# A three-layer transformer kernel: the up projections of layer 0 as one stream with the first scores among them, key rotation on GpSimd, squares of x0 to x3 folded to 256 columns

## The chip, the core and the metric

The kernel runs as one launch on one core of one Trainium2 chip. The metric is device time in microseconds, 991.06 us as the median of 3 runs of the kernel before (990.77 to 992.12). All weights are read from device memory once, as float32.

## What is computed

Two blocks are computed one after the other on 256 tokens of 1024 features. The change touches layer 0 of the first block, whose mixer is latent attention, and the norms before the projections of both layers. Cut to that:

```
x0 = x
h = rms_norm(x, g);  a = h @ w_a;  cq, ckv, kr = split(a, [384, 640])
q  = (rms_norm(cq,  g_q ) @ w_uq ).reshape(B, S, 8, 128 + 64)
kv = (rms_norm(ckv, g_kv) @ w_ukv).reshape(B, S, 8, 128 + 128)
q_rope = apply_rope(q[..., 128:]);  k_rope = apply_rope(kr)     # 64 wide, k_rope shared by the heads
s = (q_nope . k_nope + q_rope . k_rope) * 192 ** -0.5
y = softmax(mask(s)) @ v @ w_o
x1 = x + rms_norm(y, g);  z = swiglu(rms_norm(x1) )
x2 = x1 + rms_norm(z, g);  layer 1 likewise gives x3 and x4
```

An rms norm needs the sum of squares over the features, and features lie on partitions, so each such sum is a matmul with a matrix of ones.

## The kernel before

Activations lie transposed, features on the 128 partitions and the 256 tokens along the row. Every weight tile is 128 x 128 (a *unit* here). To keep float32 accuracy, a weight unit is used as a high part and a low part: ScalarE rounds it to `whi` (line 883), VectorE subtracts to give `wlo` (line 1343), and TensorE issues three matmuls of 256 columns for each unit, high x high, high x low and low x high (lines 495, 496, 501; for values with tokens as output rows, lines 550, 551, 556, of 512 columns for four units at once). The activation has the same two parts (`cqh`, `cql`; `oh`, `ol`).

Weights arrive in *pieces* of 16 units, in the order of the table `STREAM`, through four raw buffers and three buffers for the two parts. SyncE issues the load of a piece when VectorE has made the low parts of the piece four before it. ScalarE makes high parts of a piece when TensorE has used up the piece three before it. In layer 0 pieces 4 to 8 are `wuk` (keys, 16 units), `wuq` (queries, 16), `wuv` (values, 16), `wuq` (16), `wuq` (4). Pieces 9 to 12 are `wo0`.

Every engine has its own program, written out in order, with semaphore waits between them. In layer 0 all four engine programs walk one list that `_order0` and `_mixed` make (lines 141 to 195): it runs over the projection units and puts the attention steps of the four head pairs among them where a credit and a distance in units allow it. The steps of a pair are `scores` (line 625), softmax (`biased`, `exps`, `normal`), `turn` (the transposes, line 635), `values` (line 651) and `chunk` (lines 941 and 1425), which gives two units' worth of input for `wo0`. Before that list TensorE does all of `wuk` by itself, and then the list starts with 16 units of `wuq` and 6 of the 8 token blocks of `wuv`, before the first scores.

VectorE evicts a projection from PSUM with the norm's factor (`scaled_out`, lines 1436), two chunks of 256 columns at a time. Rotation of keys and of queries is `rotate`, six VectorE instructions of 256 columns (lines 1446 to 1453). The sum of squares: ScalarE makes the squares of pairs of feature chunks (128 x 512), VectorE adds them up (`square_sum`, line 1373), and TensorE multiplies the 512 columns by ones in two float32 matmuls of 256 columns (line 591). For y and z sums a `fold` (line 1379) first adds the two halves on VectorE, so one matmul does. Where token-wise factors are wanted as well (`columns`, lines 602 to 605), four matmuls of one column follow.

## Time and profile before

The profiled execution took 990.73 us, and its span of instructions 988.6 us, so 2.1 us lie around it. The median of the runs is 0.33 us above the profiled execution.

| stretch (us) | what | TensorE busy | VectorE busy | ScalarE busy | granted clock |
|---|---|---|---|---|---|
| 0 to 988.6 | all | 959.7 (97%) | 721.8 (73%) | 542.7 (55%) | 0.997 |
| 10 to 20 | first projection | 7.55 | 6.49 | 6.99 | 0.84 |
| 33.37 to 51.92 | up projections | 18.25 of 18.55 | 18.34 | 9.62 | 1.00 |
| 51.92 to 76.27 | attention among the rest of them | 20.76 of 24.35 | 16.25 | 10.23 | 1.00 |
| 76.27 to 108.34 | attention among the output projection | 31.57 of 32.07 | 17.00 | 16.64 | 1.00 |

GpSimd is busy for 17.3 us of the whole span. A share of busy time is an average over stages, so the table is to be read by stage. A matmul's record is longer than the distance to the next one, because matmuls are pipelined: in a steady row a record is 0.28 us and the next starts 0.12 us after it.

### The profile page before, as it was taken

To read this page: it belongs to the slowest core of one execution; us is meant where nothing else is said; L and a number is where in the kernel's file an instruction comes from. 1 tells how busy PE (TensorE), PEld (TensorE's weight loads), DVE (VectorE), ACT (ScalarE), POOL (GpSimd) and SP (SyncE) were. 2 spreads that over 40 slices of the span, in tenths; PEclk is the share of its full clock that TensorE was granted. 3 is DMA by queue.
4 is the path that set the end of the run, shared out by engine and by line. 5 is a ranking of instruction groups with operands and counts; after the bars stand their busy time and mean duration, and the time that the engine had idled before them with its cause. 6 is when DMAs were issued, how large, how long until landed. Compare 5 with 4: busy or idle time off the path is not lost.

```text
span 988.6 us, 18855 instructions
## 1 busy us (share of the span) xinstructions
PE 959.7 (97%) x7951; PEld 923.9 (93%) x7951; DVE 721.8 (73%) x1342; ACT 542.7 (55%) x837; POOL 17.3 (2%) x48
## 2 busy tenths in 40 slices
PE   6999999999999999999999999999999999999997
PEld 6978999999998988799999998898999999999996
DVE  5965788887657877699878888646654879888653
ACT  6635565454436556565545444546755567676542
POOL 0000000000000000000000000000130000000000
PEclk9999999999999999999999999999999999999999
DMA  7433467676664742438666883543333545555521
GB/s 288 182 128 128 193 221 280 225 252 259 263 212 154 269 147 109 171 146 323 247 265 256 328 317 122 214 175 125 129 131 130 209 171 186 199 185 199 212 89 43
DMA packets 28452, 194.71 MB, mean 197 GB/s; under 512 B 3280, under 2 KB 3536, under 8 KB 5456
## 3 DMA queue, kind: packets, MB, share of 16 engines
q1 hardware_dynamic: 28368, 193.51, 52.7%
q8 instruction: 63, 1.03, 0.4%
q14 instruction: 21, 0.17, 0.0%
HBM read 192.45 MB, written 1.05 MB: 196 GB/s over the span
## 4 chain that ended last, share of the span: by engine, by line
PE 85%; DVE 7%; ACT 5%; issue 2%; DMA 1%; SPq 1%; POOL 0%; DVEq 0%; ACTq 0%
PE bank L495 24%; PE bank L496 23%; PE bank L501 23%; DVE s_wlo L1343 2%; PE bank L625 2%; PE bank L651 2%; ACT s_whi L883 2%; PE bank L556 2%; PE bank L550 2%; PE bank L551 1%; PE bank L515 1%; PE bank L522 1%; PE bank L516 1%; PE bank L635 1%; DMA s_raw<-in_wa 1%
## 5 line engine op out<-in xcount | busy, mean ns | idle before, releaser
L1343 DVE TENSOR_TENSOR s_wlo<-s_raw,s_whi 128x512 fp32r<-128x512 f32 (+1 forms) x364 | 371.3, 1061 | 141.1 <-ACT s_whi L883 140.7
L883 ACT ACTIVATE s_whi<-s_raw 128x1024 fp32r<-128x1024 f32 (+2 forms) x233 | 305.3, 1336 | 212.2 <-PE bank L501 198.2
L495 PE MATMUL bank<-s_hh,s_whi 128*128 128x256 f32 x1400 | 393.6, 281 | 0.4 <-DVE s_hl L1425 0.2
L496 PE MATMUL bank<-s_hl,s_whi 128*128 128x256 f32 x1400 | 387.6, 277 | 0.0
L501 PE MATMUL bank<-s_hh,s_wlo 128*128 128x256 f32 x1383 | 382.8, 277 | 0.0
L495 PEld LDWEIGHTS bank<-s_hh,s_whi 128*128 128x128 f32 x1400 | 263.3, 188 | 6.2 <-issue 5.1
L496 PEld LDWEIGHTS bank<-s_hl,s_whi 128*128 128x128 f32 x1400 | 263.1, 188 | 0.1
L501 PEld LDWEIGHTS bank<-s_hh,s_wlo 128*128 128x128 f32 x1383 | 259.8, 188 | 0.0
L495 PE MATMUL bank<-s_ph,s_whi 128*128 128x256 f32 x528 | 146.4, 277 | 0.0
L496 PE MATMUL bank<-s_pl,s_whi 128*128 128x256 f32 x528 | 145.8, 276 | 0.0
L501 PE MATMUL bank<-s_ph,s_wlo 128*128 128x256 f32 x516 | 142.5, 276 | 0.0
L496 PEld LDWEIGHTS bank<-s_pl,s_whi 128*128 128x128 f32 x528 | 99.2, 188 | 0.0
L495 PEld LDWEIGHTS bank<-s_ph,s_whi 128*128 128x128 f32 x528 | 99.2, 188 | 0.0
L501 PEld LDWEIGHTS bank<-s_ph,s_wlo 128*128 128x128 f32 x516 | 96.9, 188 | 0.0
L1358 DVE CUSTOM_DVE_ANT_0 s_raw<-s_raw,s_adacc 128x1024 f32<-128x1024 f32 x48 | 56.8, 1221 | 0.0
L515 PE MATMUL bank<-s_hh,s_whi 128*128 128x256 f32 x160 | 41.8, 294 | 11.6 <-DVE s_wlo L1343 7.1
L515 PEld LDWEIGHTS bank<-s_hh,s_whi 128*128 128x128 f32 x160 | 31.7, 198 | 12.8 <-issue 7.7
L516 PE MATMUL bank<-s_hh,s_wlo 128*128 128x256 f32 x160 | 40.8, 288 | 0.0
L495 PE MATMUL bank<-s_oh,s_whi 128*128 128x256 f32 x128 | 36.9, 288 | 2.4 <-DVE s_ol L1425 2.2
L1594 DVE TENSOR_TENSOR s_tmp<-bank,s_R 128x256 f32<-128x256 f32 x44 | 18.6, 422 | 26.2 <-PE bank L501 21.0
L496 PE MATMUL bank<-s_ol,s_whi 128*128 128x256 f32 x128 | 35.8, 280 | 0.0
L501 PE MATMUL bank<-s_oh,s_wlo 128*128 128x256 f32 x128 | 35.8, 280 | 0.0
(237 smaller groups left out, 1278.9 us busy)
## 6 DMA issues: line engine op xcount, KB each, us to landing
s_raw<-in_gu SPq DMA_DIRECT2D x44, 1024.0 KB, 4.9
s_raw<-in_dn SPq DMA_DIRECT2D x33, 1024.0 KB, 4.8
s_raw<-in_wada SPq DMA_DIRECT2D x24, 1024.0 KB, 5.1
s_raw<-in_up SPq DMA_DIRECT2D x22, 1024.0 KB, 4.8
s_raw<-in_wo SPq DMA_DIRECT2D x8, 1024.0 KB, 4.8
...
```

Of the source, the lines that this page charges most:

```text
L495: e.matmul(out, hi, xh[:, k, :], start=first, stop=False, skip_group_check=True)
L496: e.matmul(out, hi, xl[:, k, :], start=False, stop=False, skip_group_check=True)
L501: m = e.matmul(out, lo, xh[:, k, :], start=False, stop=last, skip_group_check=True)
L515: e.matmul(out, hi, xh[:, k, :], start=k == 0 and j % 2 == 0, stop=False, skip_group_check=True)
L516: e.matmul(out, lo, xh[:, k, :], start=False, stop=False, skip_group_check=True)
L550: e.matmul(out, xh[:, k, xk], hi, start=k == 0, stop=False)
L556: m = e.matmul(out, xl[:, k, xk], hi, start=False, stop=k == nk - 1)
L625: m = e.matmul(pair_banks[a][:, cols_], x[:, blk * P:(blk + 1) * P], y[:, 0:rows], start=i == 0 and blk == 0, stop=last, skip_group_check= ...
L651: m = e.matmul(out, v, probs[:, a, keys], start=first, stop=kb == 1, skip_group_check=True)
L883: e.activation(whi[w % SPLIT][:, at], raw[p % RAW][:, at], ACT.Copy).then_inc(S.hi.tick((w, c0)), 1)
L1343: e.tensor_tensor(wlo[s][:, at], raw[p % RAW][:, at], whi[s][:, at].bitcast(F32), ALU.subtract).then_inc(S.lo.tick((i, j), (i, "all")), 1)
L1358: m = e.tensor_tensor_reduce(out=src, in0=src, in1=cact[:, :], scale=1.0, scalar=0.0, op0=ALU.mult, op1=ALU.add, accum_out=modv[:, j:j + 1])
```

## The change

Five things change.

The pieces 4 to 8 now hold one list `MLA` of 68 units in the order in which they are used: 4 `wuk`, 12 `wuq`, 4 `wuk`, 12 `wuq`, 16 `wuv`, 4 `wuk`, 6 `wuq`, 4 `wuk`, 6 `wuq`. Sizes and number of the pieces are as before. Only the first four units of `wuk` stand ahead of the list of steps.

The steps of the pairs are placed by other paces and distances (`PACE0`, `PAIR0`, `AFTER0`). The list was up to the first scores: 16 `wuq`, 6 token blocks of `wuv`; it is: 12 `wuq` (4 to 15 of the stream), 4 `wuk`, 8 `wuq`. The sums for q stand after three units of `wuq`.

The keys' rotation leaves VectorE and is six GpSimd instructions, with one wait between the first four and the last two, and a semaphore of its own.

VectorE makes the low parts of the third piece of the stream ahead of the first eviction of `wuk`.

For x0, x1, x2 and x3 VectorE folds the two halves, and TensorE has one matmul where it had two; for x2 also two matmuls of one column where it had four.

```diff
-STREAM = [("wa", 56), ("wuk", 16), ("wuq", 16), ("wuv", 16), ("wuq", 20), ("wo0", 64), ("gu0", 352), ("dn0", 176),
+MLA = ([("wuk", i) for i in range(4)] + [("wuq", i) for i in range(12)] +
+       [("wuk", i) for i in range(4, 8)] + [("wuq", i) for i in range(12, 24)] + [("wuv", i) for i in range(16)] +
+       [("wuk", i) for i in range(8, 12)] + [("wuq", i) for i in range(24, 30)] +
+       [("wuk", i) for i in range(12, 16)] + [("wuq", i) for i in range(30, 36)])
+STREAM = [("wa", 56), ("mla", 68), ("wo0", 64), ("gu0", 352), ("dn0", 176),
...
+PACE0 = {"wuk": 0.72, "wuq": 0.84, "wuv": 0.2, "wo0": 0.26}
+PAIR0 = (18, 18, 44, 44)
+AFTER0 = {**AFTER, "exp": ("scores", 9), "scale": ("exp", 3), "values": ("turn1", 7), "chunk": ("values", 0)}
...
             tiles("wuk", 0, 2, 2, cqh, cql, "cq", 4, S.dve_out)
             sums("kv", 6, columns=True)
-            tiles("wuk", 2, 2, 2, cqh, cql, "cq", 5, S.dve_out)
-            sums("q", 7)
-            for n in (4, 6):
-                tiles("wuk", n, 2, 2, cqh, cql, "cq", (0, 1)[n // 2 - 2], S.dve_out)
...
+                    if i == 3:
+                        sums("q", 7)
...
-                    q.wait_ge(S.rot, "k")
+                    q.wait_ge(S.rot_k, "k")
...
-                        sums({0: "x1", 1: "x3"}[layer], 0)
+                        sums({0: "x1", 1: "x3"}[layer], 0, acc=1)
...
-            q.wait_ge(S.dve_out, ("cq", 6))
-            rotate(tmp[3][:, :], tmp[4][:, :], A0.K[:, 8, :], A0.K[:, 9, :], "k")
             lo_all(_used_up("wa", 48) + SPLIT)
-            for n in (0, 2, 4, 6):
-                scaled_out("wuk", n, 2, Rs[1], "kv", lambda m: A0.K[:, m, :])
-                if n == 2:
-                    lo_all(_used_up("wa", 56) + SPLIT)
+            lo_all(_used_up("wa", 56) + SPLIT)
+            scaled_out("wuk", 0, 2, Rs[1], "kv", lambda m: A0.K[:, m, :])
...
             for i, b in ((1, 0), (2, 3), (3, 2)):
                 square_sum("x3", i, sqb[b])
+            fold("x3")
             lo_all(_used_up("gu1", 16) + SPLIT)
...
+            q.wait_ge(S.dve_out, ("cq", 6))
+            e.tensor_tensor(tmp[0][:, :], tmp[4][:, :], sinb, ALU.mult)
+            e.tensor_tensor(tmp[1][:, :], tmp[3][:, :], sinb, ALU.mult)
+            e.tensor_tensor(A0.K[:, 8, :], tmp[3][:, :], cosb, ALU.mult)
+            e.tensor_tensor(A0.K[:, 9, :], tmp[4][:, :], cosb, ALU.mult).then_inc(S.rot_k.tick("products"), 1)
+            q.wait_ge(S.rot_k, "products")
+            e.tensor_tensor(A0.K[:, 8, :], A0.K[:, 8, :], tmp[0][:, :], ALU.subtract)
+            e.tensor_tensor(A0.K[:, 9, :], A0.K[:, 9, :], tmp[1][:, :], ALU.add).then_inc(S.rot_k.tick("k"), 1)
```

How instructions stand now. First VectorE between the last part of the first projection (`s_tmp<-bank3`) and the queries' eviction (`s_Q0<-bank2` is the chunks that are rotated; `s_K0` are keys). In the kernel before:

```order
L1520 TENSOR_TENSOR s_tmp<-bank3,s_R0 128x256 x2
L1446 TENSOR_TENSOR s_tmp<-s_tmp,s_adacc 128x256
L1447 TENSOR_TENSOR s_tmp<-s_tmp,s_adacc 128x256
L1449 TENSOR_TENSOR s_K0<-s_tmp,s_adacc 128x256
L1450 TENSOR_TENSOR s_K0<-s_tmp,s_adacc 128x256
L1452 TENSOR_TENSOR s_K0<-s_K0,s_tmp 128x256
L1453 TENSOR_TENSOR s_K0<-s_K0,s_tmp 128x256
L1343 TENSOR_TENSOR s_wlo2<-s_raw1,s_whi2 128x512 x4
L1436 TENSOR_TENSOR s_K0<-bank4,s_R1 128x256 x2
L1436 TENSOR_TENSOR s_K0<-bank5,s_R1 128x256 x2
L1343 TENSOR_TENSOR s_wlo0<-s_raw2,s_whi0 128x512 x4
L1436 TENSOR_TENSOR s_K0<-bank0,s_R1 128x256 x2
```

In the changed kernel at the same place:

```order
L1545 TENSOR_TENSOR s_tmp<-bank3,s_R0 128x256 x2
L1367 TENSOR_TENSOR s_wlo2<-s_raw1,s_whi2 128x512 x4
L1367 TENSOR_TENSOR s_wlo0<-s_raw2,s_whi0 128x512 x4
L1460 TENSOR_TENSOR s_K0<-bank4,s_R1 128x256 x2
L1460 TENSOR_TENSOR s_Q0<-bank2,s_R2 128x256 x2
L1470 TENSOR_TENSOR s_tmp<-s_Q0,s_adacc 128x256
L1471 TENSOR_TENSOR s_tmp<-s_Q0,s_adacc 128x256
L1473 TENSOR_TENSOR s_Q0<-s_Q0,s_adacc 128x256
L1474 TENSOR_TENSOR s_Q0<-s_Q0,s_adacc 128x256
L1476 TENSOR_TENSOR s_Q0<-s_Q0,s_tmp 128x256
L1477 TENSOR_TENSOR s_Q0<-s_Q0,s_tmp 128x256
L1460 TENSOR_TENSOR s_Q0<-bank3,s_R2 128x256 x2
```

The six rotation rows of the keys are gone, eight weight parts stand in one row, and of the four evictions of keys ahead of the queries' first one is left; the other three stand further down.

TensorE around the first scores (`s_K,s_Q`), of before, with a token block of `wuv` (lines 550 to 556) ahead of them and another behind:

```order
L550 MATMUL bank<-s_whi,s_cqh 128x512 [waits dve_evicted]
L551 MATMUL bank<-s_wlo,s_cqh 128x512
L556 MATMUL bank<-s_whi,s_cql 128x512
L625 MATMUL bank<-s_K,s_Q 128x128 [waits rope_made,dve_evicted]
L625 MATMUL bank<-s_K,s_Q 128x128
L625 MATMUL bank<-s_K,s_Q 128x256 x2
L625 MATMUL bank<-s_K,s_Q 128x128 x2
L625 MATMUL bank<-s_K,s_Q 128x256 x2
L625 MATMUL bank<-s_K,s_Q 128x128 x2
L625 MATMUL bank<-s_K,s_Q 128x256 x2
L550 MATMUL bank<-s_whi,s_cqh 128x512 [waits weight_low_made]
```

and of the changed kernel, where a unit of `wuq` stands ahead of them and four more units and then all of `wuv` behind (what was line 625 is 642 now):

```order
L511 MATMUL bank<-s_cqh,s_whi 128x256
L512 MATMUL bank<-s_cql,s_whi 128x256
L517 MATMUL bank<-s_cqh,s_wlo 128x256
L642 MATMUL bank<-s_K,s_Q 128x128 [waits rope_made,key_rope_made,dve_evicted]
L642 MATMUL bank<-s_K,s_Q 128x128
L642 MATMUL bank<-s_K,s_Q 128x256 x2
L642 MATMUL bank<-s_K,s_Q 128x128 x2
L642 MATMUL bank<-s_K,s_Q 128x256 x2
L642 MATMUL bank<-s_K,s_Q 128x128 x2
L642 MATMUL bank<-s_K,s_Q 128x256 x2
L511 MATMUL bank<-s_cqh,s_whi 128x256 [waits weight_low_made]
```

The first scores moved ahead of the token blocks, and wait for one more semaphore, that of the rotated keys.

VectorE at the squares of x3, of before and of the changed kernel (`s_wlo2<-s_raw0` is the fourth piece of the first matrix of the feed-forward part, `s_tmp<-bank5` its first output):

```order
L1358 ISA s_raw3,s_modv<-s_raw3,s_adacc 128x1024
L1358 ISA s_modv 128x1
L1373 TENSOR_TENSOR s_sqacc0<-s_sqacc0,s_yb 128x512 x3
L1343 TENSOR_TENSOR s_wlo2<-s_raw0,s_whi2 128x2048
L1594 TENSOR_TENSOR s_tmp<-bank5,s_R2 128x256
```

```order
L1382 ISA s_raw3,s_modv<-s_raw3,s_adacc 128x1024
L1382 ISA s_modv 128x1
L1397 TENSOR_TENSOR s_sqacc0<-s_sqacc0,s_yb 128x512 x3
L1403 TENSOR_TENSOR s_sqacc0<-s_sqacc0 128x256
L1367 TENSOR_TENSOR s_wlo2<-s_raw0,s_whi2 128x2048
L1622 TENSOR_TENSOR s_tmp<-bank5,s_R2 128x256
```

A fold stands between the square sums and the weight piece.

## Rows read from the trace of the kernel before

**Rows 1.** Who TensorE waited for, whole span: total us, times, longest.

```profile
PE bank L495 <- DVE s_ol L1425: 2.2, 2, 1.8
...
PE bank L625 <- DVE s_Q L1436: 2.1, 3, 1.3
```

**Rows 2.** TensorE in time order: start, us, line, [idle before it].

```profile
16.90 0.55 PE L515 MATMUL bank<-s_hh,s_whi 128*128 128x256 f32 x1 [2.29 <-ACT s_hh L1000]
...
33.37 0.28 PE L495 MATMUL bank<-s_cqh,s_whi 128*128 128x256 f32 x1
...
34.79 1.03 PE L591 MATMUL bank<-s_sqacc,s_ones 128*128 128x256 f32 x4
...
47.31 0.40 PE L550 MATMUL bank<-s_whi,s_cqh 128*128 128x512 f32 x1
...
51.92 3.09 PE L625 MATMUL bank<-s_K,s_Q 128*128 128x128 f32 x24 [0.31 <-DVE s_Q L1436]
...
76.27 0.38 PE L495 MATMUL bank<-s_oh,s_whi 128*128 128x256 f32 x1 [1.79 <-DVE s_ol L1425]
```

**Rows 3.** VectorE in time order, from the first squares to the first scores.

```profile
23.72 3.70 DVE L1343 TENSOR_TENSOR s_wlo<-s_raw,s_whi 128x512 fp32r<-128x512 f32 x6
...
35.14 0.75 DVE L1520 TENSOR_TENSOR s_tmp<-bank,s_R 128x256 f32<-128x256 f32 x2
...
38.19 2.49 DVE L1343 TENSOR_TENSOR s_wlo<-s_raw,s_whi 128x512 fp32r<-128x512 f32 x4
...
40.60 1.41 DVE L1436 TENSOR_TENSOR s_K<-bank,s_R 128x256 f32<-128x256 f32 x4
...
47.47 0.75 DVE L1436 TENSOR_TENSOR s_Q<-bank,s_R 128x256 f32<-128x256 f32 x2
...
50.52 0.68 DVE L1343 TENSOR_TENSOR s_wlo<-s_raw,s_whi 128x512 fp32r<-128x512 f32 x1
```

**Rows 4.** ScalarE: the high parts of the piece that is used third.

```profile
37.47 1.99 ACT L883 ACTIVATE s_whi<-s_raw 128x1024 fp32r<-128x1024 f32 x2
```

**Rows 5.** GpSimd in time order: instructions that read SBUF.

```profile
403.15 1.95 POOL L1927 TENSOR_SCALAR_AFFINE_SELECT s_bias<-s_bias 128x2048 f32<-128x2048 f32 x1 [294.51 <-DMA s_bias<-in_relm]
...
706.44 0.59 POOL L1931 TENSOR_SCALAR_AFFINE_SELECT s_S<-s_S 128x128 f32<-128x128 f32 x1 [3.94 <-ACT s_S L1235]
...
709.04 0.29 POOL L1933 TENSOR_SCALAR_AFFINE_SELECT s_PT<-s_PT 128x128 f32<-128x128 f32 x1
```

**Rows 6.** VectorE beside and away from GpSimd's selects.

```profile
700.60 1.02 DVE L1798 TENSOR_TENSOR s_PT<-s_S,s_PT 128x384 f32<-128x384 f32 x2
...
706.19 1.38 DVE L1343 TENSOR_TENSOR s_wlo<-s_raw,s_whi 128x512 fp32r<-128x512 f32 x2
...
707.49 1.20 DVE L1798 TENSOR_TENSOR s_PT<-s_S,s_PT 128x384 f32<-128x384 f32 x2
...
714.16 1.30 DVE L1343 TENSOR_TENSOR s_wlo<-s_raw,s_whi 128x512 fp32r<-128x512 f32 x2
```

**Rows 7.** TensorE: sums of x2 and x3, and the matmul behind each.

```profile
315.86 1.02 PE L591 MATMUL bank<-s_sqacc,s_ones 128*128 128x256 f32 x4
...
317.54 0.48 PE L550 MATMUL bank<-s_whi,s_hh 128*128 128x512 f32 x1
...
435.52 1.03 PE L591 MATMUL bank<-s_sqacc,s_ones 128*128 128x256 f32 x4
...
436.69 0.36 PE L495 MATMUL bank<-s_hh,s_whi 128*128 128x256 f32 x1
```

**Rows 8.** VectorE: a fold, and what follows the square sums of x1 to x3.

```profile
109.40 0.42 DVE L1379 TENSOR_TENSOR s_sqacc<-s_sqacc 128x256 f32<-128x256 f32 x1
...
132.55 0.42 DVE L1594 TENSOR_TENSOR s_tmp<-bank,s_R 128x256 f32<-128x256 f32 x1 [3.72 <-issue]
...
320.92 2.50 DVE L1343 TENSOR_TENSOR s_wlo<-s_raw,s_whi 128x512 fp32r<-128x512 f32 x4 [3.15 <-ACT s_whi L883]
...
434.25 2.29 DVE L1343 TENSOR_TENSOR s_wlo<-s_raw,s_whi 128x2048 fp32r<-128x2048 f32 x1
```

More of the change, by code:

```diff
@@ L138, in _stick_steps, with _mixed @@
             yield "keep", p
-def _mixed(units, steps, paces, pair_at, chunk_name, per=1):
+def _mixed(units, steps, paces, pair_at, chunk_name, per=1, after=AFTER):
     steps, ahead, at, made, credit = iter(steps), [], {}, set(), 0.0
@@ L159, in ready @@
         else:
-            need, tiles = (AFTER[name][0], i), AFTER[name][1]
+            need, tiles = (after[name][0], i), after[name][1]
         return need in at and n >= at[need] + tiles
@@ L192, in _order0 @@
 def _order0():
-    units = _units("wuq")[:16] + [("wuv", g) for g in range(8)] + _units("wuq")[16:] + _units("wo0")
-    return _mixed(units, _soft_steps(range(4)), {"wuq": 0.3, "wuv": 0.6, "wo0": 0.3},
-                  lambda p: ("wuq", (17, 29, 35)[p - 1]) if p else ("wuv", 0), "wo0", 2)
+    units = [(name, i // 2 if name == "wuv" else i) for name, i in MLA[4:] if name != "wuv" or i % 2 == 0] + _units("wo0")
+    return _mixed(units, _soft_steps(range(4)), PACE0, lambda p: units[PAIR0[p]], "wo0", 2, AFTER0)
 def _order1():
@@ L573, in tokens @@
                     if k == 2 and norm is not None:
-                        sums(norm, 4, columns=True)
+                        sums(norm, 4, acc=1, columns=True)
             def sums(s, b, late=(), acc=2, columns=False):
@@ L602, in sums @@
                     for b in range(2):
-                        e.matmul(out[:, T + b:T + b + 1], sq[:, b * P:(b + 1) * P], ones[:, 0:1], start=True, stop=False)
-                        m = e.matmul(out[:, T + b:T + b + 1], sq[:, T + b * P:T + (b + 1) * P], ones[:, 0:1],
-                                     start=False, stop=True)
+                        for half in range(acc):
+                            at = half * T + b * P
+                            m = e.matmul(out[:, T + b:T + b + 1], sq[:, at:at + P], ones[:, 0:1], start=half == 0,
+                                         stop=half == acc - 1)
                 m.then_inc(S.sums.tick(s), 1)
@@ L684, in tensor_program @@
             for step, i in _order0():
-                if step == "wuq":
+                if step == "wuk":
+                    n, k = i // 2, i % 2
+                    if n % 2 == 0 and k == 0:
+                        bank_of["wuk", n] = (4, 0, 1, 3)[n // 2]
+                        take(bank_of["wuk", n], S.dve_out, ("wuk", n))
+                    q.wait_ge(S.xlo, ("cq", k))
+                    product("wuk", i, banks[bank_of["wuk", n - n % 2]][:, (n % 2) * T:(n % 2 + 1) * T], cqh, cql, k,
+                            k == 0, k == 1, ("wuk", n - 1) if n % 2 == 1 and k == 1 else None)
+                elif step == "wuq":
                     n, k = i // 3, i % 3
+                    if i == 3:
+                        sums("q", 7)
                     if n % 2 == 0 and k == 0:
-                        bank_of["wuq", n] = (2, 3, 0, 1, 2, 3)[n // 2]
+                        bank_of["wuq", n] = (2, 3, 1, 2, 0, 2)[n // 2]
                         take(bank_of["wuq", n], S.dve_out, ("wuq", n))
@@ L1510, in vector_program @@
                 square_sum("x0", i, sqv[i])
+            fold("x0")
             lo_all(_used_up("wa", 16) + SPLIT)
```

53 lines of the change are left out of this document (36 added, 17 removed).

## The prediction

> **What bounds the kernel now.** I read the table of stretches first, then the waits, then the time order of each engine. TensorE is busy for 97% of the span, so time can only come from three places: matmuls that go, waits of TensorE that go, and clock. The waits in the stage that the change rewrites are few: TensorE waits three times for evicted queries (2.1 us in all, the longest 1.3) and twice for the low part of the attention output (2.2 in all, the longest 1.8) [rows 1]. A unit costs 0.353 us: four stand between 33.37 and 34.79 (1.42 us), so 0.118 for each matmul, while a record is 0.28 long [rows 2]. A gap that is printed as idle is thus about 0.16 us longer in truth, and the five waits cost 4.3 + 5 x 0.16 = 5.1 us. This is all that a better order of the stage can give, since its matmuls stay the same.
>
> Who makes TensorE late? Up to 51.92 VectorE has no pause, and the scores wait for it [rows 2, 3]: it does the keys' rotation, the evictions and all low parts ahead of the queries that the first scores need. Behind 51.92 the queries' evictions stand behind softmax work. The longest wait, 1.79 at 76.27, is another thing: ScalarE copies twice and VectorE subtracts, with no work for TensorE beside it.
>
> **The stage, step by step.** Both kernels are alike up to the sums for kv. Up to 47.31 TensorE had 28 units and the sums for q behind them; ahead of the first scores it now has 24 units and the same sums. So it comes to the scores at 47.31 - 4 x 0.353 = 45.9 [rows 2]. What stands ready then?
>
> VectorE: its last eviction of the first projection begins at 35.14 and takes two steps of 0.34 us. The fold of x0 ahead of it costs 0.42 (at 109.40 [rows 8]), so it is free at 36.2. Then eight low parts of 0.60 each (a row of four is 2.49 long, of which 0.09 is the tail of the last, at 38.19 [rows 3]) to 41.0; ScalarE has the last high parts at 37.47 + 1.99 = 39.5, ahead of the seventh part, no wait [rows 4]. Keys out, two steps of 0.34 (four take 1.41 less the tail [rows 3]): 41.7. Queries out and rotated: 50.52 - 47.47 = 3.05, so 44.75 [rows 3]. The next queries out, 0.75: 45.5, and with the semaphore 45.6. That is 0.3 us ahead of TensorE. In the kernel before the same eviction came 0.31 + 0.16 us late although TensorE came 5.5 us later: four evictions, the rotation and weight parts went first.
>
> GpSimd: it starts at 36.2 and must be done by 45.9, so it has 9.7 us for six instructions. The trace has none of their kind. The nearest rows are selects with one input: 128 columns in 0.29 us, 2048 columns in 1.95, so 0.86 ns for each column and 0.18 fixed [rows 5]. Two inputs of 256 columns are between 0.40 (one pass) and 0.62 (two passes); the longest row, 1.95, is the upper end. Beside VectorE instructions with two SBUF inputs a select took 0.59 in place of 0.29 [rows 5, 6], so 0.3 more for each. I take 0.62 + 0.3, and 5.5 us for six, done near 41.8. The keys are not late.
>
> What does VectorE pay? In the same rows 6 its instructions beside four selects took 1.38 against 1.30 and 1.20 against 1.02: 0.26 us for four selects, 0.065 each. A select reads 128 columns once; a product reads 256 twice, four times as much. I take 0.26 each, 1.6 us for six; the low end is 6 x 0.065 = 0.4, the high end that VectorE stands still for all of each, 6 x 0.62 = 3.7. All six fall beside the eight low parts, which have both inputs in SBUF. With 1.6 the scores wait 1.6 - 0.3 = 1.3 us (0.1 to 3.4).
>
> The Trainium skill (SBUF — State Buffer, "Who interferes with whom") says that a VectorE instruction with two SBUF inputs contends with a GpSimd instruction that reads SBUF, and that the winner holds the shared pair for its whole instruction. By that rule the price is the high end. The rows agree that both engines get slower, 0.29 to 0.59 and 1.02 to 1.20, but not that VectorE loses all of it. The same skill (GPSIMD Engine Reference, 3.1) gives 4497 ns for a sum of 2048 columns; scaled to 256 that would be an estimate of 0.56 us, no run here shows it.
>
> Further on, with durations of rows and the new order. The turn of pair 0 comes 1.4 us behind the second scores and needs VectorE's reads of their banks, 768 columns, at 0.34 us for 256 some 1.0 us, more with four instructions, and semaphores: 0.2 late. The third scores come when the eviction of their queries ends: 0.1. The first unit of the output projection needs the chunk of pair 0. Before, TensorE stood 1.79 + 0.16 us there with nothing beside it [rows 2]; now four units, 1.4 us, stand beside the same chain, so 0.5 is left. The fourth turn needs its bank freed behind seven weight parts: 0.1. In sum 0.9 (0.3 to 1.6).
>
> Stage: -5.1 + 1.3 + 0.9 = -2.9 us. SyncE's loads have the same sizes and wait for the same distances, and the low parts that release them come earlier, so I put nothing there. Key rotation on TensorE's side costs nothing but the wait above.
>
> **The folds.** Two float32 matmuls of 256 columns take 1.03 us less the tail of 0.16, 0.87, so one is 0.43 [rows 7]. Behind the sums of x2 the next matmul starts at 317.54, 1.68 after the first: 0.81 for four matmuls of one column, and two of them go, 0.4. The fold costs VectorE 0.42.
> x0: the six low parts at 23.72 follow the squares [rows 3], and the first of them is needed right behind the sums. It comes 0.42 later, so what TensorE saves it waits away: 0 (-0.4 to +0.2).
> x1: VectorE has 3.72 us of idle time behind it, up to 132.55 [rows 8]: -0.43.
> x2: 3.15 us of idle time, up to 320.92 [rows 8]: -0.43 - 0.4 = -0.83.
> x3: here the cover is gone already. The sums start at 435.52 and the next unit should follow at 436.39, but it starts at 436.69 [rows 7], just behind the weight piece that VectorE begins at 434.25 and ends at 434.25 + 2.29 = 436.54 [rows 8]. The fold moves that piece 0.42 later. TensorE saves 0.43 and then waits 0.3 + 0.43 + 0.42: the unit comes 0.4 later than before. +0.4, low end -0.43 if that unit doesn't wait for the piece.
> In sum -0.9.
>
> **Sum.** 990.73 - 2.9 - 0.9 = 986.9 us for an execution like the profiled one (its span 988.6 and 2.1 around it), and 0.3 more for the median: 987.2 us.
>
> **Rivals.**
> A. GpSimd and VectorE shut each other out for whole instructions. For it: the select's 0.59. Against it: VectorE's 0.26 us for four. VectorE is late by 3.7 and the scores by 3.4; if the clock falls as it did at 16.90, where after 2.29 us without work a matmul took 0.55 us in place of 0.28, the level of 1.2 GHz [rows 2], up to 1.6 us more is lost in the next 3.3 us. Sum -5.1 + 3.4 + 0.9 - 0.9 = -1.7: 989.4, with the clock 991.
> B. The softmax chain becomes the bound. ScalarE now makes eight high parts' worth of weights (four instructions of 1.0 us) ahead of the third pair's exponentials, and a turn, a bank or a chunk comes later than I placed it. For it: the slacks that I found there are 0 to 0.3 us. Against it: the long chains have units beside them. At 1.5 us: 988.7.
> C. The slower side: the rotated keys come late. The place is the first scores, the price is 1 us for each us past 45.9, and nothing else of the stage is ready to be done in the meantime, since the matmuls stand in order. At 1.95 us for each, the longest GpSimd row, and 0.3 to 0.6 lost to VectorE, six take 15 us and end at 51.3: 5.4 late, with the clock 7. Then -5.1 + 7 + 0.9 - 0.9 = +1.9: 993.2. It decides from 2.2 us for one instruction on. Against it: two inputs of 256 columns are 512 columns, a quarter of that row.
> D. All goes better: 0.4 us of contention, x0 gives 0.4, the small waits 0.3. -5.1 + 0.1 + 0.3 - 1.3 = -6.0: 985.1.
>
> **How the numbers follow.** The forecast 0.52 (986 to 988.5), A 0.18, B 0.12, C 0.06, D 0.12. The range from 985.0 to 991.0 leaves out C, half of the clock's case of A, and a little beyond D: some 0.13. This kernel's measurement tells a change of about 2 us, 0.2%, from none. Faster than 989.1: the forecast, D, B mostly, and a third of A, 0.75. Within: the rest of A and B, and a part of C, 0.20. Slower: 0.05.
>
> **What the changed profile would show.** Right: the first scores near 46 to 47.5 with VectorE's query eviction as their releaser; low parts in rows longer than 0.62 while GpSimd works between 36 and 42; the last unit of the output projection 2.9 us ahead of before; the matmul behind the sums of x3 waiting about 1.1 us, those of x1 and x2 not. Wrong: scores released by GpSimd; a wait in the chunk of pair 0 as long as before; TensorE at 1.2 GHz near 50 us; or the matmul behind the sums of x3 close behind them.

## The result and the profile after

The changed kernel takes 986.57 us in the median of 7 runs (985.39 to 989.32), the kernel before 990.77 (989.57 to 992.12) beside it. The ratio is 0.9964, with a 95% interval of 0.995 to 0.9977. In a second comparison, with 11 runs of the change, it is 0.9966 (0.9954 to 0.9978). Forecast were 987.2 us and "faster". One run of all, of the kernel with the keys' rotation on VectorE (1389.34 us at a granted clock of 0.65), was in a slow state and is left out. The profiled execution took 986.47 us (forecast 986.9), its span is 983.3 us.

The line numbers have moved. In the kernel after, L511, L512 and L517 are the matmuls of a unit (L495, L496 and L501 before), L607 and L621 the sums of squares, L642 the scores, L1367 the low parts, L1460 the evictions of keys and queries.

Who TensorE waited for from 10 to 110 us, in the kernel after (us in total, times, longest), against [rows 1]:

```profile
PE bank L607 <- DVE s_sqacc L1403: 1.8, 1, 1.8
PE bank L642 <- DVE s_Q L1460: 1.4, 1, 1.4
...
PE bank L511 <- DVE s_ol L1449: 0.4, 1, 0.4
```

Three waits for queries have become one, two waits for the low part of the attention output one, and there is a new one at the sums of x0. In time order TensorE shows (start, us, line, idle before it), against [rows 2]:

```profile
23.69 0.67 PE L607 MATMUL bank<-s_sqacc,s_ones 128*128 128x256 f32 x2 [1.82 <-DVE s_sqacc L1403]
24.20 0.38 PE L511 MATMUL bank<-s_hh,s_whi 128*128 128x256 f32 x1
...
35.46 1.03 PE L607 MATMUL bank<-s_sqacc,s_ones 128*128 128x256 f32 x4
...
47.80 1.36 PE L642 MATMUL bank<-s_K,s_Q 128*128 128x128 f32 x7 [1.35 <-DVE s_Q L1460]
...
73.91 0.38 PE L511 MATMUL bank<-s_oh,s_whi 128*128 128x256 f32 x1 [0.42 <-DVE s_ol L1449]
...
105.83 1.13 PE L612 MATMUL bank<-s_yb,s_ones 128*128 128x256 f32 x4 [0.69 <-ACT s_yb L927]
```

From the sums for kv (35.46) to the first sums for y0 (105.83) the stage takes 70.37 us. Before it took 74.52 (34.79 to 109.31). That is 4.15 of the 5.3 us by which the span is shorter; the folds at x1 and x2 give 1.4 (behind the sums of x1 0.43, behind those of x2 1.00); at the start 0.7 us went the other way, since the sums for kv come 11.77 us behind those of x0 and came 10.77 behind them before, with those of x0 0.3 earlier. The last 0.4 lies behind the sums of z1. The profiled times are only 4.3 us apart, since 3.2 us lie around the span in place of 2.1. There the granted clock was at its lower level, 1.2 GHz, at another place: before right behind the wait at 16.90 [rows 2], after in the stretch from 25 us on. The table of stretches of the kernel after (us, then busy time and instructions of PE, PEld, DVE, ACT and POOL, then the granted clock, DMA share, GB/s):

```profile
25.00:29.00 4.00, 4.00 (x24) 4.00 (x23) 3.70 (x9) 2.15 (x6) 0.00 (x0) 0.58 0.51 143
...
35.46:47.80 12.34, 10.99 (x90) 10.59 (x89) 11.04 (x22) 5.59 (x8) 8.13 (x6) 1.00 0.53 190
```

VectorE up to the first scores, in the kernel after, against [rows 3] (`s_wlo` are low parts, `s_K` and `s_Q` evictions of keys and queries):

```profile
35.53 2.48 DVE L1367 TENSOR_TENSOR s_wlo<-s_raw,s_whi 128x512 fp32r<-128x512 f32 x4
39.22 4.15 DVE L1367 TENSOR_TENSOR s_wlo<-s_raw,s_whi 128x512 fp32r<-128x512 f32 x4 [1.20 <-ACT s_whi L906]
43.29 0.74 DVE L1460 TENSOR_TENSOR s_K<-bank,s_R 128x256 f32<-128x256 f32 x2
...
47.00 0.75 DVE L1460 TENSOR_TENSOR s_Q<-bank,s_R 128x256 f32<-128x256 f32 x2
```

And GpSimd, which rotates the keys beside it:

```profile
35.77 2.85 POOL L1956 TENSOR_TENSOR s_tmp<-s_tmp,s_adacc 128x256 f32<-128x256 f32 x1 [33.23 <-DVE s_tmp L1545]
38.58 0.73 POOL L1957 TENSOR_TENSOR s_tmp<-s_tmp,s_adacc 128x256 f32<-128x256 f32 x1
39.27 1.25 POOL L1958 TENSOR_TENSOR s_K<-s_tmp,s_adacc 128x256 f32<-128x256 f32 x1
40.48 1.19 POOL L1959 TENSOR_TENSOR s_K<-s_tmp,s_adacc 128x256 f32<-128x256 f32 x1
41.74 1.07 POOL L1961 TENSOR_TENSOR s_K<-s_K,s_tmp 128x256 f32<-128x256 f32 x1
42.78 1.20 POOL L1962 TENSOR_TENSOR s_K<-s_K,s_tmp 128x256 f32<-128x256 f32 x1
```

Four low parts took 2.48 us while one GpSimd instruction lasted 2.85, then four took 4.15 while GpSimd needed 1.07 to 1.25 for each. The one instruction in which VectorE stood idle took 0.73. That is the puzzle for the experiments. The second row comes 1.20 us late because of ScalarE, whose high parts of this piece stand behind a function that waits for TensorE's sums for kv (L621):

```profile
37.31 0.48 ACT L934 ACTIVATE s_L<-bank,s_epsc 128x258 f32<-128x258 f32 x1 [2.07 <-PE bank L621]
...
38.15 1.99 ACT L906 ACTIVATE s_whi<-s_raw 128x1024 fp32r<-128x1024 f32 x2
```

The sums of x2 and x3 in the kernel after, against [rows 7]:

```profile
311.80 0.59 PE L607 MATMUL bank<-s_sqacc,s_ones 128*128 128x256 f32 x2
312.23 0.50 PE L621 MATMUL bank<-s_ones,s_sqacc 128*128 128x1 f32 x4
312.59 0.47 PE L566 MATMUL bank<-s_whi,s_hh 128*128 128x512 f32 x1
...
430.67 0.59 PE L607 MATMUL bank<-s_sqacc,s_ones 128*128 128x256 f32 x2
432.09 0.36 PE L511 MATMUL bank<-s_hh,s_whi 128*128 128x256 f32 x1 [0.83 <-DVE s_wlo L1367]
```

From the sums of x2 to the next matmul it is 0.79 us (1.68 before). From those of x3 it is 1.42 (1.17 before).

### The profile page after: what moved, and what is told of

It reads as the page before. It is cut to its first block, busy times and chain, and to the rows that moved or that the text cites. A ratio compares the mean times of both kernels' runs of the same rounds, so it can differ in the third digit from the quotient of the medians.

```text
span 983.3 us, 18834 instructions
## 1 busy us (share of the span) xinstructions
PE 954.9 (97%) x7939; PEld 920.2 (94%) x7939; DVE 722.6 (73%) x1340; ACT 542.3 (55%) x837; POOL 25.4 (3%) x54
## 4 chain that ended last, share of the span: by engine, by line
PE 88%; ACT 4%; DVE 4%; issue 1%; DMA 1%; SPq 1%; POOL 0%; DVEq 0%; ACTq 0%
PE bank L511 25%; PE bank L512 24%; PE bank L517 23%; PE bank L642 2%; PE bank L668 2%; PE bank L572 2%; PE bank L566 2%; ACT s_whi L906 2%; PE bank L567 2%; DVE s_wlo L1367 1%; PE bank L531 1%; PE bank L538 1%; PE bank L532 1%; PE bank L652 1%; DMA s_raw<-in_wa 1%
## 5 line engine op out<-in xcount | busy, mean ns | idle before, releaser
L1367 DVE TENSOR_TENSOR s_wlo<-s_raw,s_whi 128x512 fp32r<-128x512 f32 (+1 forms) x364 | 372.7, 1065 | 141.6 <-ACT s_whi L906 141.4
L511 PE MATMUL bank<-s_hh,s_whi 128*128 128x256 f32 x1400 | 394.1, 282 | 1.2 <-DVE s_wlo L1367 0.8
L512 PE MATMUL bank<-s_hl,s_whi 128*128 128x256 f32 x1400 | 388.1, 277 | 0.0
L517 PE MATMUL bank<-s_hh,s_wlo 128*128 128x256 f32 x1383 | 383.4, 277 | 0.0
L511 PEld LDWEIGHTS bank<-s_hh,s_whi 128*128 128x128 f32 x1400 | 263.9, 189 | 7.5 <-issue 6.2
L512 PEld LDWEIGHTS bank<-s_hl,s_whi 128*128 128x128 f32 x1400 | 264.0, 189 | 0.1
L517 PEld LDWEIGHTS bank<-s_hh,s_wlo 128*128 128x128 f32 x1383 | 260.5, 188 | 0.0
L511 PE MATMUL bank<-s_ph,s_whi 128*128 128x256 f32 x528 | 146.4, 277 | 0.0
L512 PE MATMUL bank<-s_pl,s_whi 128*128 128x256 f32 x528 | 145.8, 276 | 0.0
L517 PE MATMUL bank<-s_ph,s_wlo 128*128 128x256 f32 x516 | 142.5, 276 | 0.0
L512 PEld LDWEIGHTS bank<-s_pl,s_whi 128*128 128x128 f32 x528 | 99.2, 188 | 0.0
L511 PEld LDWEIGHTS bank<-s_ph,s_whi 128*128 128x128 f32 x528 | 99.2, 188 | 0.0
L517 PEld LDWEIGHTS bank<-s_ph,s_wlo 128*128 128x128 f32 x516 | 96.9, 188 | 0.0
L531 PE MATMUL bank<-s_hh,s_whi 128*128 128x256 f32 x160 | 40.4, 288 | 10.9 <-DVE s_wlo L1367 7.5
L511 PE MATMUL bank<-s_oh,s_whi 128*128 128x256 f32 x128 | 36.8, 287 | 0.6 <-DVE s_ol L1449 0.4
L512 PE MATMUL bank<-s_ol,s_whi 128*128 128x256 f32 x128 | 35.7, 279 | 0.0
L517 PE MATMUL bank<-s_oh,s_wlo 128*128 128x256 f32 x128 | 35.7, 279 | 0.0
```

What stands on the lines that cost most here:

```text
L511: e.matmul(out, hi, xh[:, k, :], start=first, stop=False, skip_group_check=True)
L512: e.matmul(out, hi, xl[:, k, :], start=False, stop=False, skip_group_check=True)
L517: m = e.matmul(out, lo, xh[:, k, :], start=False, stop=last, skip_group_check=True)
L531: e.matmul(out, hi, xh[:, k, :], start=k == 0 and j % 2 == 0, stop=False, skip_group_check=True)
L1367: e.tensor_tensor(wlo[s][:, at], raw[p % RAW][:, at], whi[s][:, at].bitcast(F32), ALU.subtract).then_inc(S.lo.tick((i, j), (i, "all")), 1)
```

## The experiments

All are edits of the changed kernel. Single times scatter by one or two us, more than most of the effects, so the main measure is a length in the trace of one profiled execution of each kernel: the stage from the sums for kv to those for y0, and the wait ahead of the first scores in it.

| kernel | median us (runs) | ratio to before (95% interval) | stage us | wait at first scores, printed |
|---|---|---|---|---|
| before | 990.77 (7) | 1 | 74.52 | 0.31 |
| changed | 986.57 (7) | 0.9964 (0.9950 to 0.9977) | 70.37 | 1.35 |
| changed, again | 987.60 (11) | 0.9966 (0.9954 to 0.9978) | 74.11 | 1.85 |
| keys' rotation on VectorE | 988.93 (10, ratio from 9) | 0.9980 (0.9970 to 0.9991) | 71.37 | 2.08 |
| no rotation of keys | 985.00 (4) | 0.9939 (0.9924 to 0.9953) | 68.97 | none |
| early GpSimd product | 985.86 (6) | 0.9954 (0.9939 to 0.9969) | 70.99 | 1.82 |
| later parts | 984.30 (4) | 0.9934 (0.9919 to 0.9949) | 69.04 | none |
| later parts, rotation on VectorE | 984.32 (5) | 0.9937 (0.9925 to 0.9949) | 69.05 | none |
| no folds | 986.40 (8) | 0.9966 (0.9954 to 0.9978) | 70.69 | 1.55 |
| no fold x0, x3 | 985.63 (12) | 0.9957 (0.9945 to 0.9969) | 75.86 | 1.90 |
| later parts, no fold x0, x3 | 983.29 (5) | 0.9926 (0.9914 to 0.9938) | 69.08 | none |
| later parts, no fold x0 | 983.88 (5) | 0.9928 (0.9915 to 0.9941) | 69.00 | none |
| later parts, no folds | 985.30 (5) | 0.9938 (0.9924 to 0.9952) | 69.03 | none |

The stages of 74.11 and 75.86 hold a stretch at 1.2 GHz, of which more below. Without a wait at the scores the stage is 68.97 to 69.08 us in all six kernels; what it is longer in the other kernels with the new order, but for these two, is their wait, within 0.3 us.

**Keys' rotation back on VectorE.**

```diff
+            q.wait_ge(S.dve_out, ("cq", 6))
+            rotate(tmp[3][:, :], tmp[4][:, :], A0.K[:, 8, :], A0.K[:, 9, :], "k")
             lo_all(_used_up("wa", 48) + SPLIT)
...
-            e.tensor_tensor(A0.K[:, 9, :], A0.K[:, 9, :], tmp[1][:, :], ALU.add).then_inc(S.rot_k.tick("k"), 1)
```

> The keys' rotation goes back to VectorE, right behind the last eviction of the first projection; all else is as in the changed kernel. Theory S (the two engines share, and each gets slower): VectorE gains 1.66 us, since its second row of four low parts takes 2.49 again in place of 4.15, and the 1.20 us that it stood idle ahead of that row take up half of the 2.3 us of the rotation. Then evictions, rotation of the queries and the first scores come 0.5 us earlier than in the changed kernel: scores at 47.3, a printed wait of 0.8 us in place of 1.35. The time is that of the changed kernel or 0.5 us less (986.0 to 986.6). Rival R (the move to GpSimd took 2.3 us off VectorE, as it was meant to): the scores come 1 to 2.3 us later, wait 2.3 to 3.6, time 987.5 to 989.

VectorE in this kernel:

```profile
35.22 0.75 DVE L1545 TENSOR_TENSOR s_tmp<-bank,s_R 128x256 f32<-128x256 f32 x2
...
38.27 4.89 DVE L1367 TENSOR_TENSOR s_wlo<-s_raw,s_whi 128x512 fp32r<-128x512 f32 x8
...
46.80 0.74 DVE L1460 TENSOR_TENSOR s_Q<-bank,s_R 128x256 f32<-128x256 f32 x2
```

From the end of the first projection's evictions to the second eviction of queries VectorE needed 10.9 us (35.89 to 46.80), against 11.47 in the changed kernel (35.53 to 47.00), of which 1.20 are the idle time. But the two profiles differ in their start. Here the sums for kv came at 34.40, 10.4 us behind those of x0, and not 11.8, so the scores waited longer, 2.08. The fair partner is the changed kernel run again (further down), which has its sums at the same place and no idle time: there VectorE needed 10.55 us (36.01 to 46.56) and the scores waited 1.85. Of the 2.4 us that the rotation takes on VectorE, 2.0 come back, because the rotation of the queries no longer meets GpSimd. So beside a like execution the move to GpSimd is worth 0.2 to 0.4 us. Theory S's gain could only come in an execution with the idle time; that was not profiled with this kernel. The wait is above S's 0.8 and below rival R's 2.3 to 3.6. The median, 988.93, is at the upper end of R's 987.5 to 989; nine runs go from 986.21 to 990.73, four of them with a granted clock of 0.993 to 0.995. The ratio's interval lies above that of the kernel with the early product (0.9939 to 0.9969), which was run beside it; the 3 us between their medians are more than the traces explain.

**No rotation of the keys.** GpSimd writes a constant into the two chunks.

```diff
+            e.memset(A0.K[:, 8:10, :], 0.5).then_inc(S.rot_k.tick("k"), 1)
```

> GpSimd writes a constant into the two rotated chunks of the keys and reads nothing; the rotation of the keys is left out, so the scores are those of other keys. Theory S: the second row of four low parts takes 2.5 us, VectorE is ready with the queries 1.6 us earlier and the wait ahead of the first scores (printed 1.35) is gone or under 0.2: the stage from the sums for kv to those for y0 takes 68.9 us in place of 70.37, time 985.1. Rival W (the second row was long for another reason, such as ScalarE's high parts beside it): it stays above 3.5 us, the wait stays at 1 us or more, and the time is that of the changed kernel.

VectorE's rows in this kernel:

```profile
36.23 2.49 DVE L1367 TENSOR_TENSOR s_wlo<-s_raw,s_whi 128x512 fp32r<-128x512 f32 x4
39.91 2.50 DVE L1367 TENSOR_TENSOR s_wlo<-s_raw,s_whi 128x512 fp32r<-128x512 f32 x4 [1.20 <-ACT s_whi L906]
42.33 0.75 DVE L1460 TENSOR_TENSOR s_K<-bank,s_R 128x256 f32<-128x256 f32 x2
...
46.04 0.74 DVE L1460 TENSOR_TENSOR s_Q<-bank,s_R 128x256 f32<-128x256 f32 x2
```

The second row is 2.50 in place of 4.15, with the same 1.20 us of idle time ahead of it, the path is 1.66 us shorter, the wait is gone, the stage is 68.97 (68.9 expected) and the median 985.0 (985.1 expected). GpSimd's instructions beside VectorE were the whole of the 1.66 us.

**An early product on GpSimd.**

```diff
+            q.wait_ge(S.const, "ready")
+            e.tensor_tensor(A0.K[:, 8, 0:2], ident[:, 0:2], tri[:, 2:4], ALU.mult).then_inc(S.rot_k.tick("warm"), 1)
+            q.wait_ge(S.rot_k, "warm")
             q.wait_ge(S.trig, "cos")
```

> GpSimd does one product of 2 columns some 30 us earlier, long before the rotation. The first of its six instructions was 2.85 us long, the others 0.73 to 1.25. Theory C (the first instruction of this kind pays a start of about 2 us): it now takes 0.7 to 1.25, GpSimd is done near 42.0 in place of 43.98, fewer of its instructions lie beside VectorE's second row of four low parts (3.3 to 3.7 in place of 4.15), more beside the first row, where the 1.20 us of idle time behind it take that up; the first scores come 0.5 to 0.8 earlier. Theory L (VectorE's row of four at 35.53 to 38.01 kept GpSimd out; 38.01 + 0.61 is just where the first one ends): it still takes 2.8 us and nothing moves.

Theory C falls: the first large instruction is not shorter but longer, 5.24 us. VectorE's and GpSimd's rows in this kernel:

```profile
35.97 4.89 DVE L1367 TENSOR_TENSOR s_wlo<-s_raw,s_whi 128x512 fp32r<-128x512 f32 x8
40.79 0.74 DVE L1460 TENSOR_TENSOR s_K<-bank,s_R 128x256 f32<-128x256 f32 x2
...
42.23 0.93 DVE L1470 TENSOR_TENSOR s_tmp<-s_Q,s_adacc 128x256 f32<-128x256 f32 x1
43.08 0.96 DVE L1471 TENSOR_TENSOR s_tmp<-s_Q,s_adacc 128x256 f32<-128x256 f32 x1
```

```profile
36.23 5.24 POOL L1959 TENSOR_TENSOR s_tmp<-s_tmp,s_adacc 128x256 f32<-128x256 f32 x1 [33.40 <-DVE s_tmp L1545]
41.42 0.74 POOL L1960 TENSOR_TENSOR s_tmp<-s_tmp,s_adacc 128x256 f32<-128x256 f32 x1
42.12 0.75 POOL L1961 TENSOR_TENSOR s_K<-s_tmp,s_adacc 128x256 f32<-128x256 f32 x1
42.82 0.93 POOL L1962 TENSOR_TENSOR s_K<-s_tmp,s_adacc 128x256 f32<-128x256 f32 x1
```

VectorE did eight low parts without a pause and without any loss (4.89, as in the kernel without GpSimd's work), up to 40.86, and GpSimd's instruction ended at 41.47, 0.61 later. In the changed kernel VectorE's row of four ended at 38.01 and GpSimd's instruction at 38.62, 0.61 later again. In the kernel with later parts the two are 38.98 and 39.58. This is theory L: an unbroken row of low parts on VectorE keeps GpSimd out, until the row pauses or is over. In the changed kernel a pause followed, here and in the kernel with later parts it was the evictions of keys, without a pause. Whether the row ends after four or after eight parts isn't due to the early product: the changed kernel itself, run again, showed 5.26 us beside a row of eight with 4.89. It hangs on ScalarE's third piece, which is there in time or, when TensorE's sums for kv are late, not.

The scores came at 47.31, 0.5 earlier than in the changed kernel's first profile, as C had it, but not for C's reason: the changed kernel run again has them at 47.36 without the product. They waited 1.82 us. In place of low parts the rotation of the queries was slowed: its first four instructions took 0.85 to 0.96 us, the last two 0.42.

**Later parts.** The low parts of the third piece stand behind the second eviction of queries.

```diff
-            lo_all(_used_up("wa", 56) + SPLIT)
             scaled_out("wuk", 0, 2, Rs[1], "kv", lambda m: A0.K[:, m, :])
...
-                    if i % 2 == 1 and i % 6 != 5:
+                    if i % 2 == 1 and i % 6 != 5 and i > 11:
...
-                        lo_part(_mla_used(step, i) + SPLIT)
+                        if i == 11:
+                            lo_all(_mla_used(step, i) + SPLIT)
+                        if i > 11:
+                            lo_part(_mla_used(step, i) + SPLIT)
```

> The third weight piece of the stage gets its low parts behind the second eviction of queries, not ahead of the first keys: four parts less ahead of the first scores. If the scores' wait of 1.35 us (printed) comes from these parts and from GpSimd beside them, VectorE evicts keys at 38.3, queries at 41.0 when their scale is there, and the second queries at 45.5 to 46.2; the wait falls to 0.2 or less and the stage (70.37 us) is 1.3 us shorter, 985.3. Contention then falls on the rotation of the queries, 2.3 us long, up to 3.9. Rival: the parts are late for their own units or delay the second keys, and a wait of 0.5 to 1.5 us stands 3 to 5 us behind the scores: the stage as long as before, 986.5.

VectorE and TensorE in this kernel:

```profile
40.58 0.76 DVE L1460 TENSOR_TENSOR s_Q<-bank,s_R 128x256 f32<-128x256 f32 x2 [0.93 <-ACT s_R L937]
...
44.78 0.75 DVE L1460 TENSOR_TENSOR s_Q<-bank,s_R 128x256 f32<-128x256 f32 x2
45.45 3.08 DVE L1367 TENSOR_TENSOR s_wlo<-s_raw,s_whi 128x512 fp32r<-128x512 f32 x5
```

```profile
45.70 0.28 PE L517 MATMUL bank<-s_cqh,s_wlo 128*128 128x256 f32 x1
45.82 1.04 PE L642 MATMUL bank<-s_K,s_Q 128*128 128x128 f32 x6
```

The scores follow the unit ahead of them without a gap. The stage is 1.33 us shorter and no wait turned up behind it: the rival falls. The median is 984.30, the four runs lie within 0.7 us.

**Later parts with the rotation on VectorE.** Both edits above together.

> Third piece's low parts behind the second queries, and the keys' rotation on VectorE, ahead of the second piece's low parts. With the parts gone VectorE no longer stands idle for ScalarE, so the 2.3 us of the rotation are paid: the low parts end near 41.2, keys and queries out at 42.6, the queries' rotation undisturbed (2.3 us in place of 3.5), second queries out at 46.2 in place of 45.5 (for sums for kv at 35.0). The first scores wait 0.4 to 0.8 us; 984.8 to 985.1. This would say that the move to GpSimd is worth 0.5 us once the order lets it, and nothing or less where four low parts lie beside it. Rival: no wait, 984.3, GpSimd worth nothing in either order.

The rival was right: no wait, the stage as long (69.05), the time the same (984.32). The expectation's own sum was off by 1.2 us: low parts to 41.3, queries out at 41.9 to 42.6, 2.3 us of rotation, is 45.0 and not 46.2. VectorE's row says 44.96, where with GpSimd's help it was 44.78; counted from VectorE's last eviction of the first projection that is 9.17 against 8.95 us. What GpSimd takes off VectorE, 2.3 us, is nearly lost again to its instructions beside the queries' rotation (1.1 us) and to VectorE's idle time ahead of the queries' scale (0.93). The 0.2 us that are left fall where TensorE doesn't wait. So in this order the move to GpSimd gave nothing.

**Folds.** The kernels without folds use two sum matmuls of 256 columns (four records in the trace), as before the change. For x0:

```diff
-            sums("x0", 7, acc=1)
+            sums("x0", 7)
...
-            fold("x0")
```

> No square is folded in x0 to x3; the new order and the keys' rotation on GpSimd stay. Theory F: at x1 0.43 and at x2 0.83 to 0.99 us come back, at x3 0.25 goes, x0 gives nothing: 1.1 us more than the changed kernel, 987.7, and from the stage alone, measured in the trace from the sums for kv to those for y0, the same 71.3 within 0.3. Rival: the folds at x1 and x2 only move waits, and the time is that of the changed kernel.

By the trace, from the sums of y0 to those of z1 it takes 491.8 us (106.58 to 598.36) in place of 490.6 (106.80 to 597.40): the 1.2 us came back, as expected. The median didn't show it (986.40, 987.7 expected): theory F by the trace, inconclusive by the time. The stage is 70.69 us, 0.3 more than the changed kernel's 70.37; the 71.3 of the expectation, called "the same", is neither.

> The squares of x0 and x3 are summed by two matmuls of 256 columns again, without the fold; x1 and x2 stay folded. Theory F (the fold of x3 costs as the prediction says, since a weight piece stands behind it on VectorE): from the sums of x3 to the next unit 1.17 us in place of 1.42. At x0 the sums come 0.4 earlier and take 0.43 longer: the unit behind them starts where it did, within 0.2. Time of the changed kernel less 0.3 (986.3). Rival X (x0 decides: TensorE stood 1.82 us there for the fold, printed, and the clock fell to 1.2 GHz behind it): without the fold this wait is 0.4 us shorter, the fall comes less often, and the time is 0.7 to 2 us less (984.6 to 985.9).

Median 985.63, at the upper end of rival X. The profiled execution was the 991.52 us one, so its stage can't be compared. What the fold at x0 costs, all the traces tell: from VectorE's first square sum to the unit behind the sums it is 3.39 to 3.40 us in the seven executions with the fold (20.80 to 24.20 in the changed kernel) and 3.17 to 3.22 in the six without (21.66 to 24.84 in the kernel below), whether TensorE was at the sums early or late. So the fold costs 0.2 us. The matmuls save less here than at x1: with the fold the unit starts 0.51 us behind the begin of the sums, without it 0.68 to 0.75. Sums and next unit in the kernel without folds:

```profile
24.09 1.10 PE L607 MATMUL bank<-s_sqacc,s_ones 128*128 128x256 f32 x4 [1.16 <-DVE s_sqacc L1397]
24.84 0.47 PE L511 MATMUL bank<-s_hh,s_whi 128*128 128x256 f32 x1
```

The next three have the narrow spread of the kernels without a wait at the scores, so they were to split the folds by time.

> Third piece's low parts behind the second queries, and no fold at x0 and x3. If the two gains are of separate places they add: no wait at the first scores, 1.17 us at x3 in place of 1.25, so 984.0 to 984.3, 0.1 to 0.3 below the kernel with the later parts alone (984.3). Rival X: 983.0 to 983.5, by x0.

983.29 us (983.11 to 983.49), 1.0 below the kernel with the later parts alone: more than 0.1 to 0.3, and in rival X's range. But the cause that X names isn't shown. In the two profiled executions 0.7 us of the difference lie ahead of the fold already (VectorE's square sums begin at 21.04 here and at 21.76 there), and each kernel has only one profile, so the start's scatter can't be told from the order.

> Later third piece, x0 not folded, x1, x2 and x3 folded. It parts the 1.0 us between the kernel with the later parts (984.30) and the one without folds at x0 and x3 besides (983.29). Theory F (x3 costs 0.3 by its unit behind the sums, x0 up to 0.4): 983.5 to 983.7. Rival (the fold at x3 costs nothing in the end, since from the sums of x3 to those of z1 the traces show 166.7 us with it and without): 983.3, and x0 alone is worth the 1.0.

983.88 (983.10 to 984.15), above both answers and between the two kernels that it was to part; the difference to 983.29 is within the spread. So the times don't split the 1.0 us. The traces decide for the rival on x3: from the sums of x3 to those of z1 it takes 166.73 us in the changed kernel, 166.74 in the kernel before, 166.72 in the one without folds at x0 and x3, although the unit behind the sums starts 1.42, 1.17 and 0.95 us behind them (the last two kernels are without the fold at x3). In the two profiled kernels with later parts and the fold at x3 it is 166.55 and 166.57.

> Later third piece and no fold in x0 to x3. Against the kernel without folds at x0 and x3 (983.29) the folds at x1 and x2 go: by the steps of the prediction 0.43 and 0.83 us, by the trace of the changed kernel 0.43 and 0.99: 984.5 to 984.7. Rival (the ends of the kernels without and with folds in the earlier order, 986.4 and 986.6, tell of no gain): 983.3 to 983.7.

985.30 (983.42 and 983.91, and three of 985.3 to 985.5), expected 984.5 to 984.7; what makes the two groups stays open. By the trace: from the sums of x1 to those of z0 166.50 us in place of 166.08 (0.42), from the sums of x2 to those of y1 99.71 in place of 98.90 (0.81), both against the kernel above. The folds at x1 and x2 are worth 1.2 us.

**The changed kernel again.**

> The changed kernel itself, beside the two others of this call. Two states of it are expected: where TensorE's wait of 1.4 to 1.9 us ahead of the first scores passes without a fall of the clock, 985.2 to 986.6; where the granted clock falls to 1.2 GHz behind it, some 3 to 6 us more (2 of 7 runs so far were at 988.8 and 989.3, with granted clocks of 0.995 and 0.993). The kernels with the later parts, without that wait, should show no such runs.

Five of its 11 runs have a granted clock of 0.993 to 0.995 and times of 987.60 to 989.93; the other six have 0.997 to 0.999 and 985.05 to 987.79. The profile caught one of the former (989.63 us). Its stretches behind the scores (the same columns as above):

```profile
45.00:48.00 3.00, 1.15 (x10) 0.96 (x9) 2.96 (x7) 0.00 (x0) 0.56 (x1) 1.00 0.05 19
48.00:51.00 3.00, 3.00 (x17) 2.13 (x17) 3.00 (x7) 0.00 (x0) 0.00 (x0) 0.57 0.00 0
51.00:54.00 3.00, 3.00 (x16) 2.35 (x15) 1.40 (x10) 0.00 (x0) 0.00 (x0) 0.50 0.91 279
54.00:57.00 3.00, 3.00 (x14) 2.62 (x14) 1.83 (x5) 0.63 (x1) 0.00 (x0) 0.80 0.18 74
```

TensorE stood idle for 1.85 us up to 47.36, and then worked at 1.2 GHz to about 55 us. The stage took 74.11 us, 3.1 more than with about the same wait and no fall (70.99). In the kernel without the folds of x0 and x3 the same wait of 1.90 was followed by a fall to 58 us, and the run took 991.52, some 6 us more than its neighbours. Over all kernels with this wait, 17 of the 53 runs in the ratios have a clock of 0.995 or less; of the 28 runs of the six kernels without it none has. That the fall stands behind this wait is seen in the two profiles only; for the other 15 runs it is inferred from their mean clock. Nor is the wait enough by itself. The kernel before has its wait of 1.79 us at 76.27 [rows 2] with the clock at 1.00 around it, and none of its 50 runs in these comparisons is below 0.996. What the six profiled executions with the wait show beside it: the two that fell had also run at a clock of 0.58 and 0.61 from 17 to 20 us, and the four that didn't fall had 1.00 there. Whether that matters wasn't tested.

## Why the prediction was right, and where it wasn't

**The waits of the stage: near in each term, the first by luck.** Counted by the starts of the matmuls, the stage before had 5.6 us of waits, where the prediction took 5.1 from five of them and left small ones out. After, it has 1.51 at the first scores (1.3 forecast), 0.57 at the chunk of pair 0 (0.5), 0.19 at the first turn (0.2), and none at the third scores or the fourth turn (0.1 each): 2.3, where 2.2 was forecast. That is -3.3 for -2.9.

The 1.3 us at the first scores came out because two errors cancel. Counted from the sums for kv, the prediction has VectorE's low parts begin 1.4 us behind them (36.2, with the sums at 34.79). Measured is 0.1 (35.53 and 35.46), 1.3 less, since the clock fell behind TensorE's wait at x0 and its sums came 11.77 us behind those of x0. On the other side stands the step "ahead of the seventh part, no wait": VectorE stood idle for 1.20 us, because ScalarE was held up by the same late sums. With 0.1 more of contention and TensorE 0.3 earlier than forecast (10.8 us behind its sums, not 11.1) that gives 1.5. In the executions with the sums where the prediction had them, the start and the "no wait" hold, and the wait is 1.8 to 1.9 as printed: there it was the contention, 2.0 us, that was taken too small.

**The stage as a whole: 4.15 us, not 2.9.** The rest, 0.86 us, is no wait. TensorE's matmuls of 256 columns stood 0.118 us apart before, and in most of the stretch from 36 to 47 us 0.113 after. In the kernel after, twelve starts lie between these two, 1.36 us, where it was 1.42 for twelve [rows 2]:

```profile
40.05 0.28 PE L517 MATMUL bank<-s_cqh,s_wlo 128*128 128x256 f32 x1
...
41.41 0.28 PE L517 MATMUL bank<-s_cqh,s_wlo 128*128 128x256 f32 x1
```

For the 72 matmuls ahead of the scores that is 0.3 us. What sets it I can't say: the kernel with later parts and no folds at x0 and x3 stood at 0.118 there, with the same stage of 69.1. The other 0.5 us stays open.

**The price of the contention: the right sum from the wrong parts, by luck.** The prediction took 6 x 0.26 = 1.6 us; measured are 1.66. But it is 3 x 0.55. The changed kernel's second row has four low parts: without GpSimd 2.49 us, with it 4.15. In the execution with no folds at x0 and x3 four GpSimd instructions fell into a row of eight, and it took 7.09, 4.89 + 4 x 0.55:

```profile
36.14 7.09 DVE L1367 TENSOR_TENSOR s_wlo<-s_raw,s_whi 128x512 fp32r<-128x512 f32 x8
```

So each GpSimd instruction that VectorE meets costs it 0.55 us, which is near the 0.62 of rival A and not the 0.26 of the forecast. The step that failed is "a product reads 256 twice, four times as much. I take 0.26 each": it scaled a loss of four short selects, of which the trace had no proof that all of them met VectorE's reads. Rival A failed in its count: it let all six be paid, and three or four are. In the changed kernel the first waits out VectorE's row and costs nothing, the second falls into VectorE's pause, and the last ends beside evictions, which aren't slowed. The rule weighed in the prediction (the Trainium skill, SBUF — State Buffer, "Who interferes with whom": one engine holds the shared pair for its whole instruction and the other is blocked) agrees with these rows: 0.73 us alone and 1.2 beside VectorE for GpSimd, 0.60 and 1.15 for a low part, in turns. What the rows show beside it is who gets the pair next: GpSimd's first instruction began at 35.77, and the low parts that VectorE began after that, up to 38.01, still went ahead of it.

**GpSimd's time.** Forecast 5.5 us and done near 41.8, measured 8.2 us and done at 43.98. It still had 2.3 us to spare ahead of TensorE's arrival at 46.3, so rival C (late keys) didn't decide. (C's own sum, 990.73 + 1.9 + 0.3, is 992.9 and not 993.2; nothing else rests on it.)

**Rival B** (the softmax chain) didn't come: behind the first scores only 0.19 and 0.57 us of waits are left.

**The folds.** x1: -0.43 forecast, measured -0.43. x2: -0.83 forecast, -0.81 to -1.00 measured. x3: +0.4 forecast; the next unit comes 0.25 later, for the reason given, and by the sums of z1 nothing of it is left. x0: 0 forecast, with -0.4 to +0.2 around it; measured +0.2, the upper end. The unit waits for the fold, 0.42 us on VectorE, and the matmuls give back only 0.2 of it, not 0.43.

**What was missing: the clock behind the new wait.** The prediction put the fall of the clock only into rivals A and C, behind waits of over 3 us. Measured, about a third of the runs of the kernels with a wait of 1.4 to 2.1 us ahead of the scores have a lower clock, and two profiles show the fall right behind it. The slower runs among the change's 985.1 to 989.9 are mostly these. How long the wait is hangs on the start: TensorE's sums for kv come 10.4 to 10.8 us behind those of x0, or 11.8 where it ran at 1.2 GHz in between, and VectorE doesn't follow. The forecast of the wait fits the first profile of the changed kernel, 1.35, and not the second, 1.85.

**The version that the runs point to**, later parts and no fold at x0 and x3, takes 983.29 us: 0.9926 of before (0.9914 to 0.9938), 3.3 us less than the change. From the later parts with all folds (984.30, 0.9919 to 0.9949) it isn't told apart clearly.
